# Two dense blocks on one core: three seams between products computed by token halves

## The reference, cut to what matters

```
x    += 0.5 * gate * swiglu(ada_norm(x))        # ffn 0, for latent and context
x    += gate * mixer(ada_norm(x))               # layer 0: even mixer, layer 1: odd mixer
x    += 0.5 * gate * swiglu(ada_norm(x))        # ffn 1
ada_norm(x) = x * rsqrt(mean(x*x) + eps) * g * (1 + scale) + shift
swiglu(h)   = (silu(h @ Wa) * (h @ Wb)) @ Wout
```

## Time and profile before

| | |
|---|---|
| median of 3 runs | 2419.37 us (2418.14 to 2423.27) |
| the profiled execution | 2423.33 us, its span 2421.5 us |
| TensorE, VectorE, ScalarE, GpSimd busy | 95%, 48%, 36%, 6% |
| mean granted TensorE clock | 0.973 |

### The profile page before, as it was taken

One profiled execution on the slowest core, in us unless ns is written; L12 is line 12 of the kernel. 1 busy time (PEld: TensorE's weight loads), 2 busy tenths in 40 slices (PEclk: granted clock), 3 DMA queues, 4 the chain that ended last, 5 costly groups with the idle time before them and its releaser, 6 DMA issues.

```text
span 2421.5 us, 35525 instructions
## 1 busy us (share of the span) xinstructions
PE 2310.0 (95%) x13280; PEld 1863.4 (77%) x13280; DVE 1156.7 (48%) x1943; ACT 876.3 (36%) x1399; POOL 154.0 (6%) x134
## 2 busy tenths in 40 slices
PE   6999999999999999988999999999999998988998
PEld 4777797877777778856777777778788876968998
DVE  5226375643433353376553333354343345566665
ACT  4126454632222232346443222244222234355544
POOL 0003112100000010040200000010000010000000
PEclk9999999999999999988999999999999998998999
DMA  9652543445555245400344665333233232323573
GB/s 304 198 165 81 179 133 79 148 122 173 179 178 176 86 119 155 124 9 27 105 148 146 196 183 157 104 109 94 72 117 90 79 105 69 88 70 113 164 207 116
DMA packets 514685, 312.87 MB, mean 129 GB/s; under 512 B 15899, under 2 KB 513138, under 8 KB 514454
## 3 DMA queue, kind: packets, MB, share of 16 engines
q1 hardware_dynamic: 513992, 311.33, 43.5%
q10 hardware_dynamic: 590, 0.16, 0.0%
HBM read 310.41 MB, written 1.05 MB: 129 GB/s over the span
## 4 chain that ended last, share of the span: by engine, by line
PE 86%; DVE 7%; ACT 3%; issue 2%; DMA 1%; ACTq 0%; POOL 0%; DVEq 0%; POOLq 0%
PE ps L907 68%; PE ps L949 4%; PE ps L717 4%; DVE w_lo L1551 2%; PE ps L1793 1%; ACT w_hi L1168 1%; PE ps L859 1%; PE ps L1772 1%; PE ps L2114 1%; PE ps L1780 1%; PE ps L790 1%; PE ps L811 0%; PE ps L2010 0%; DVE small L2286 0%; PE ps L728 0%
## 5 line engine op out<-in xcount | busy, mean ns | idle before, releaser
L907 PE MATMUL ps<-h_hi,w_hi 128*128 128x512 f32 (+1 forms) x2208 | 806.5, 365 | 28.3 <-DVE h_lo L1408 14.1
L907 PE MATMUL ps<-h_lo,w_hi 128*128 128x512 f32 (+1 forms) x2208 | 793.0, 359 | 0.0
L907 PE MATMUL ps<-h_hi,w_lo 128*128 128x512 f32 (+1 forms) x2208 | 792.9, 359 | 0.0
L907 PEld LDWEIGHTS ps<-h_hi,w_hi 128*128 128x128 f32 x2208 | 420.9, 191 | 126.5 <-issue 48.4
L1551 DVE TENSOR_TENSOR w_lo<-stage,w_hi 128x1024 fp32r<-128x1024 f32 x227 | 284.0, 1253 | 403.3 <-ACT w_hi L1168 402.8
L907 PEld LDWEIGHTS ps<-h_hi,w_lo 128*128 128x128 f32 x2208 | 421.0, 191 | 67.9
L907 PEld LDWEIGHTS ps<-h_lo,w_hi 128*128 128x128 f32 x2208 | 421.6, 191 | 63.7
L1168 ACT ACTIVATE w_hi<-stage 128x1024 fp32r<-128x1024 f32 x227 | 237.0, 1055 | 360.9 <-PE ps L907 245.7
L1551 DVE TENSOR_TENSOR w_lo<-deep,w_hi 128x1024 fp32r<-128x1024 f32 x184 | 225.4, 1234 | 274.5 <-ACT w_hi L1168 273.3
L907 PE MATMUL ps<-g_hi,w_hi 128*128 128x512 f32 (+1 forms) x704 | 260.2, 370 | 0.6 <-DVE w_lo L1551 0.3
L907 PE MATMUL ps<-g_hi,w_lo 128*128 128x512 f32 (+1 forms) x704 | 257.4, 366 | 0.0
(11 more groups left out here) (368 smaller groups left out, 2381.8 us busy)
## 6 DMA issues: line engine op xcount, KB each, us to landing
modw<-in_ada_w SPq DMA_DIRECT2D x72, 1024.0 KB, 5.6
stage<-in_ffn_w_in SPq DMA_DIRECT2D x88, 512.0 KB, 4.5
deep<-in_ffn_w_in SPq DMA_DIRECT2D x88, 512.0 KB, 3.8
modw<-in_w_mod SPq DMA_DIRECT2D x18, 1024.0 KB, 7.8
stage<-in_w_in SPq DMA_DIRECT2D x30, 512.0 KB, 4.7
stage<-in_ffn_w_out SPq DMA_DIRECT2D x32, 384.0 KB, 3.4
stage<-in_even_w_in SPq DMA_DIRECT2D x24, 512.0 KB, 4.0
deep<-in_ffn_w_out SPq DMA_DIRECT2D x32, 384.0 KB, 3.5
```

Of the source, the lines that this page charges most:

```text
L907: last = mm(ps[:, j, 0:b - a], w_part[wp][:, u % RING, c, :], x_part[xp][:, x, a:b], start=first and wp == xp, stop=final and wp == "lo")
```

## The change

The phase `seam` takes the place of the last two output chunks of the old projection, of the norm and of the first four units of the new one. The old chunks j=6 and 7 are computed for the latent half, then for the context half (which alone raises `unit_done`). During the context half the latent sums of squares and rstd are computed. Then the four new units run for the latent half, the second pair q=1 interleaved with chunks 4 to 7 of the first pair q=0, and after that for the context half. VectorE and ScalarE get one written order each with evacuations, weight splits and norm chunks; the latent norm issues scaled(c+1) after low(c), the context norm ahead of it. The gemm before a seam has six output chunks (its sums include a sixth square), the one after it begins four units later. The first gemm of the even mixer hosts its modulation segments in half as many units, another takes two more, the ffn's two fewer. `deep` now starts with the first new unit of seam 3.

```diff
+        def seam(tail, start, norm, dst=None):
+            units = 2 * len(tail["ks"]) + 4
+            r = {"unit_done": units, "w_hi": units, "w_ready": units, "x_done": 2, "sq_half": 4, "ms_sum": 2, "rms_ready": 2, "diag_ready": 2,
+                 "rstd_ready": 2, "t_ready": 2 * KC, "hi_ready": 2 * KC, "h_ready": 2 * KC, "bank_free0": 1, "bank_free1": 1, "bank_free2": 3, "bank_free3": 3}
+            if dst is None:
+                r.update({"x_done": 4, "sg_half": 4, "gh_hi": 4, "g_half": 2, "g_ready": 2})
+            add("seam", r, start=start, norm=norm, dst=dst, **tail)
+        def ffn(i, nt, hpers, after=None):
...
-                     sumsq="resid" if half else None, fed=not (last and i and half), peel=i and half, hper=hpers[2 * half + 1])
+                w_down = dict(w=("ffn_w_out_2", l, i), src="g", ks=(6, 5), row0=half * FH, l=l, g=2 * i)
+                if half and after:
+                    gemm(w_down.pop("w"), 0, KC - 2, "resid", tok=(0, nt), sumsq="early", **w_down)
+                    after(dict(w=("ffn_w_out_2", l, i), **w_down))
+                else:
+                    gemm(w_down.pop("w"), 0, KC, "resid", tok=(0, nt), sumsq="resid" if half else None,
+                         fed=not (last and i and half), peel=i and half, hper=hpers[2 * half + 1], **w_down)
+        w = ("even_w_in_2", 0) if l == 0 else ("odd_w_in_2", 0)
+        def into_even(tail):
+            modvec(1, 0, (1, 2))
+            seam(tail, w, (0, 1), dst=0)
+        def into_last(tail):
+            modvec(1, 1, (0, 1, 2))
+            seam(tail, ("ffn_w_in_2", 1, 0), (1, 0))
 
...
-            gemm(w, 0, 8, "copy", dst=0, hper=2)
+            gemm(w, 512, 4, "copy", dst=4, hper=4)
             add("rotary", {"roped": 1, "lam_e": 1}, half=0)
             gemm(w, 1024, 2, "tok", dst="vda")
             add("rotary", {"roped": 1}, half=1)
-            gemm(w, 1536, 4, "copy", dst=8, hper=2)
+            gemm(w, 1536, 4, "copy", dst=8, hper=4)
...
-            gemm(("even_w_out_2", 0), 0, 8, "resid", l=l, g=1, sumsq="resid")
+            tail = dict(src="h", ks=(KC,), row0=0, l=l, g=1)
+            gemm(("even_w_out_2", 0), 0, KC - 2, "resid", sumsq="early", **tail)
+            seam(dict(w=("even_w_out_2", 0), **tail), ("ffn_w_in_2", 0, 1), (0, 2))
...
+        def tn_of(v, c):
+            return tn[:, c % 6, :] if v == 0 else big3[:, 11 + 12 * (c // 2 % 2), c % 2 * SEQ:c % 2 * SEQ + SEQ]
...
-        first_deep = next(p.at("unit_done") for p in phases if p.kind == "gemm" and p.at("mod_rows") == total["mod_rows"] and p.kw["ks"] == (KC,))
+        first_deep = next(p.at("unit_done") for p in phases if p.kind == "seam" and p.at("mod_rows") == total["mod_rows"]) + 4
...
+        def sp_seam(eng, p):
+            k, u0 = p.kw, p.at("unit_done")
+            w_out, w_in = (weight(w).rearrange("(k p) n -> p k n", p=P) for w in (k["w"], k["start"]))
+            u = u0
+            for j in (6, 7):
+                for s, kc in enumerate(k["ks"]):
+                    first = k["row0"] + sum(k["ks"][:s])
+                    slot, full, _, again = arrival(u)
+                    eng.wait_ge(S("w_ready"), u - again + 1)
+                    eng.dma_start(slot[:, 0:kc, :], w_out[:, first:first + kc, j * P:j * P + P]).then_inc(full, 16)
+                    u += 1
+            if u == first_deep:
+                eng.wait_ge(S("mod_rows"), total["mod_rows"])
+            for j in range(4):
+                col = j * P if k["dst"] is not None else j // 2 * P + j % 2 * D_FF
+                slot, full, _, again = arrival(u)
+                eng.wait_ge(S("w_ready"), u - again + 1)
+                eng.dma_start(slot[:, :, :], w_in[:, 0:KC, col:col + P]).then_inc(full, 16)
+                u += 1
...
+        def pe_seam(eng, p):
+            k, u0 = p.kw, p.at("unit_done")
+            ks, per = k["ks"], len(k["ks"])
+            w_part, x_part = {"hi": w_hi, "lo": w_lo}, {"hi": h_hi, "lo": h_lo}
+            t_part = x_part if k["src"] == "h" else {"hi": g_hi, "lo": g_lo}
+            def sums(v):
+                if v == 0:
+                    for name in ("mod_sum", "mod_kept"):
+                        eng.wait_ge(S(name), p.at(name))
+                    eng.wait_ge(S("sq_used"), p.at("sq_used"))
+                eng.wait_ge(S("sq_half"), p.at("sq_half", 2 * v + 2))
+                cols = slice(v * SEQ, (v + 1) * SEQ)
+                up(pe_half_sums(v, [sqsum[:, cols], sq[:, 0, cols], sq[:, 1, cols]], True, True), "ms_sum")
+            for v in range(2):
+                cols = slice(v * SEQ, (v + 1) * SEQ)
+                for j in range(2):
+                    eng.wait_ge(S(f"bank_free{2 + j}"), p.at(f"bank_free{2 + j}", v))
+                    for s, kc in enumerate(ks):
+                        u = u0 + j * per + s
+                        if v == 0:
+                            eng.wait_ge(S("w_ready"), u + 1)
+                        for n in range(kc):
+                            x = sum(ks[:s]) + n
+                            for wp, xp in W_X:
+                                last = mm(ps[:, 2 + j, cols], w_part[wp][:, u % RING, n, :], t_part[xp][:, x, cols],
+                                          start=x == 0 and wp == xp, stop=x == sum(ks) - 1 and wp == "lo")
+                            if v and j * sum(ks) + x == 3:
+                                sums(0)
+                            if v and j * sum(ks) + x == 8:
+                                pe_half_rstd(eng, p, 0, 1)
+                        if v:
+                            up(last, "unit_done")
+                    if v == 0:
+                        up(last, "x_done")
+            u1 = u0 + 2 * per
+            turn = [(0, n) for n in range(4)] + [(q, n + 4 * (1 - q)) for n in range(4) for q in (1, 0)] + [(1, n) for n in range(4, KC)]
+            for v in range(2):
+                cols = slice(v * SEQ, (v + 1) * SEQ)
+                for q, n in turn:
+                    if q == 0:
+                        eng.wait_ge(S("h_ready"), p.at("h_ready", KC * v + n + 1))
+                    for j in range(2):
+                        u = u1 + 2 * q + j
+                        bank, part = (2 * q + v, slice(j * SEQ, (j + 1) * SEQ)) if k["dst"] is None else (2 * q + j, cols)
+                        if n == 0:
+                            if v == 0:
+                                eng.wait_ge(S("w_ready"), u + 1)
+                            eng.wait_ge(S(f"bank_free{bank}"), p.at(f"bank_free{bank}", 2 * (bank // 2)))
+                        for wp, xp in W_X:
+                            last = mm(ps[:, bank, part], w_part[wp][:, u % RING, n, :], x_part[xp][:, n, cols],
+                                      start=n == 0 and wp == xp and (k["dst"] is not None or j == 0), stop=n == KC - 1 and wp == "lo", skip_group_check=True)
+                        if n == KC - 1 and v and k["dst"] is not None:
+                            up(last, "unit_done")
+                    if n == KC - 1 and k["dst"] is None:
+                        up(last, "unit_done", by=2) if v else up(last, "x_done")
+                    if v == 0 and (q, n) == (0, 3):
+                        sums(1)
+                    if v == 0 and (q, n) == (0, 6):
+                        pe_half_rstd(eng, p, 1, 2)
...
+        def seam_splits(p):
+            return ((4,), (5,), (), (6, 7)) if len(p.kw["ks"]) == 2 else ((4,), (), (), (5,))
+        def act_seam(eng, p):
+            k, u0 = p.kw, p.at("unit_done")
+            u1 = u0 + 2 * len(k["ks"])
+            m = 2 + k["norm"][0]
+            def square(v, j):
+                eng.wait_ge(S(f"bank_free{2 + j}"), p.at(f"bank_free{2 + j}", v + 1))
+                cols = slice(v * SEQ, (v + 1) * SEQ)
+                up(act(sq[:, j, cols], resid[:, 6 + j, cols], ACT.Square), "sq_half")
+            def high(v, c):
+                eng.wait_ge(S("t_ready"), p.at("t_ready", KC * v + c + 1))
+                up(act(h_hi[:, c, v * SEQ:(v + 1) * SEQ], tn_of(v, c), ACT.Identity, bias=modT[m][:, k["norm"][1] * 24 + c, v:v + 1], scale=1.0), "hi_ready")
+            def gate(v, q):
+                cols = slice(v * SEQ, (v + 1) * SEQ)
+                eng.wait_ge(S("unit_done"), u1 + 2 * q + 2) if v else eng.wait_ge(S("x_done"), p.at("x_done", 3 + q))
+                up(act(sg[:, q, cols], ps[:, 2 * q + v, 0:SEQ], ACT.Silu), "sg_half")
+            def keep(j):
+                eng.wait_ge(S("unit_done"), u1 + j + 1)
+                up(act(big3[:, k["dst"] + j, :], ps[:, j, :], ACT.Copy), f"bank_free{j}")
+            act_split(eng, u0 + 3)
+            act(small[:, 212:213], epsc[:, :], ACT.Sqrt)
+            eng.wait_ge(S("sq_used"), p.at("sq_used"))
+            square(0, 0)
+            square(0, 1)
+            act_half_root(eng, p, 0, 1)
+            for c in range(KC):
+                if c < 4:
+                    for s in seam_splits(p)[c]:
+                        act_split(eng, u0 + s)
+                high(0, c)
```

(90 more changed lines are left out.)

37 lines of the change are left out of this document (16 added, 21 removed).

## The result

Four runs of each: 2435.73 us after (2433.45 to 2440.13) against 2420.96 before (2418.14 to 2423.27). The ratio is 1.0064, 95% interval 1.0045 to 1.0083: slower by 0.64%. Forecast was 2432.9 us, +13.5; measured +14.8. The profiled execution of the kernel after took 2440.13 us, its span 2438.3.

A forecast was written before the change was run, and what follows sets the result against it. TensorE, busy 95%, bounds the kernel; only seam gaps, 27.9 us, can be won. New work 11.55 + 1.2, stalls 23.1 and clock 5.6 make 41.4, so +13.5: 2432.9 us. Range 2416 to 2441, likeliest case 2425 to 2439.5.

The forecast's parts named there:

- The old cost and TensorE's own work: Three seams: old gaps and slow matmuls 27.9 us; new sums and rstd 11.55, halves 1.2; worth 15.2 without stalls.
- The stalls of the walk: TensorE waits at the seams from the VectorE and ScalarE queue order: 6.5 + 9.2 + 7.4 = 23.1 us.
- The fourth chunk: Chunk 3 of the latent norm, behind weight splits it does not need: stalls 4.25, 1.85, 2.95 us in seams 1 to 3.
- the bank: Seam 2, old units' context half: bank 2 evacuated only behind the split of u0+3, stall 2.3 us.
- the ends: After seams 2 and 3 the next product waits for weights whose ring slots come free late: 2.15 us each.
- Chunks 4 and 5: Latent norm chunks after the second sums, root and diagonal: stalls of 1.4, 1.35 and 1.4 us.
- The clock: Half clock after stalls: 1.6 us each for two, 0.8 each for three, 5.6 in all, bounds 0 and 14.
- the price from the earlier trace: In a late product, after a 2.52 us wait, 18 half matmuls take 3.75 us instead of 2.12, 1.63 lost.
- (a): Rival: the splits hide, queues keep up at chunk 3; sum +1.2, 2420.6 us, no change; chance 0.15.
- (b): Rival: faster, weight splits outside TensorE's path; -7.7, 2411.7 us, or 2404 with no wait left; chance 0.13.
- (c): Rival: all five stalls draw the dearest clock loss and segments cost 2; +24, 2443.4 us; chance 0.08.
- The segments: Seam 1's modulation segments, four per four units instead of two: up to 2 us if delaying a weight, taken at 0.

The follow-up runs named there:

- all orders: Kernel after with end and bank edits, weight splits just ahead of the weight's own use, one chunk scaled ahead: 2409.78 us, ratio 0.9965 to before.
- three edits: Each alone on the kernel after: weight splits behind the fourth chunk 2424.15 us; straight order at the end 2430.98; bank ahead of the split in seam 2 2432.90.
- seam 2 alone: Only the second seam runs by halves, the other two as in the kernel before: 2427.21 us, ratio 1.0024 to before.
- splits behind: Kernel after with the weight splits moved behind the fourth chunk's high and low parts: 2424.15 us, ratio 1.0018 to before.
- two kernels with reads: All orders plus, per seam, two or four VectorE reductions nobody reads, ahead of the second chunk's low op: 2414.75 us (two), 2419.68 (four).
- three small edits: Kernel after with splits behind the fourth chunk, straight order at the end and bank ahead of the split together: 2420.06 us, ratio 0.9998 to before.
- seam 3 alone: Only the third seam runs by halves, the other two as in the kernel before: 2422.25 us, ratio 1.0010 to before.
- seam 1 alone: Only the first seam runs by halves, the other two as in the kernel before: 2424.28 us, ratio 1.0022 to before.
- bank first: Kernel after, latent halves evacuated before the fourth weight's split in seam 2, ScalarE's root table loaded after the squares: 2432.90 us, ratio 1.0052 to before.
- straight end: Kernel after with the new units' context half running pair q=0 to its last chunk, then q=1: 2430.98 us, ratio 1.0044 to before.

## Why the prediction was right, and where it was not

**The old cost and TensorE's own work: right.** 27.9 us of old gaps and slow matmuls, against 11.55 + 1.2 of new work. Twelve sums matmuls hold up the next product 1.25 us (878.83, the row itself is 1.45 long) for the 1.36 forecast, halves start 0.118 us apart. The kernel with all orders checks it: 468 x 0.233 = 109.0, + 12.75 of work, + 3.0 of waits makes 124.8, and eight of its waits cost 0.16 us more than the row says, because a matmul's row is 0.28 long while the next starts 0.118 later: 126.1 against 126.6 measured. The sum holds better than its terms: the rstd matmuls take 0.25 us each in all orders instead of 0.52, so sums and rstd come to 9.3 us instead of 11.55, and in their place stand some 2.8 us of pauses of 0.1 to 0.2 us at single halves, too short for the list of waits. So halves were worth the forecast 15.2 us, less the waits.

**The stalls of the walk: right in place, a little large.** The fourth chunk 3.65, 1.43 and 2.56 us (forecast 4.25, 1.85, 2.95), the bank 2.02 (2.3), the ends 2.01 and 2.01 (2.15 each), none at the end of seam 1. The first chunks 0.50, 0.97 and 0.48 (0.85, 1.55, 0.9). Together 15.6, and 17.2 with 0.16 for each of the ten rows, against 18.95 forecast. That the order of the queue is their cause is shown: each of three edits moves operations without removing one, and the waits that it aims at go, but for 0.49 us at the fourth chunk of seam 2 and 0.26 at its sums. Of the three, only the splits' worth in time is clear of noise.

**Chunks 4 and 5: wrong in the kernel after.** 1.4, 1.35 and 1.4 us were forecast and none is there. The clock hid them: TensorE was then at its lower level and used a chunk in 2.6 us instead of 1.41. Where the clock stays up they come: 0.51 + 0.35 us in seam 2 alone, for the 1.35 forecast. (With the splits behind, seam 1 has 0.22 + 0.82 there, but in that kernel two splits stand ahead of these chunks.) The two kernels with reads agree: seam 1 has 0.24 + 0.16 us of waits there with two reads, at full clock, and none with four, at the lower.

**The clock: the term that was mis-sized.** Forecast 5.6 us: 1.6 for two stalls, 0.8 for three. Half matmuls and sums ran slow for some 27.5 us, at 0.213 instead of 0.118 each, which loses 12.2; with 1.4 and 1.5 at the ends 15.1. The step that failed is the price from the earlier trace rows, 18 half matmuls in 3.75 us, as the dear end: the stall of 2.56 in seam 3 was followed by nearly 9 us at the lower level, seam 1's and seam 2's bank wait by 8 and 7, and 1.43 us, which had got no clock term, also dropped it. Too much for chunks 4 and 5 (4.15), too little for the clock (9.5): the two errors are one thing counted in two places, and half cancelled.

**Sum.** 12.75 + 17.2 + 15.1 = 45.1, where the lengths show 153.0 - 109.0 = 44.0 and the forecast had 41.4; the 1.1 us between are not explained. Against the 137.2 of before the lengths give +15.8, against +13.5 forecast and +14.8 measured.

**The rivals.** (a), the splits hide, fell: moving them gave 11.6 us. (b), faster, did not hold for this order; but its floor of 2404 was a fair one, for with the order mended the time is 2409.8. Its point of decision, stalls and clock under 15.2, is borne out by all orders (some 5 us, faster). The three small edits have 11.9 in the profiled execution and should by it be 3 us faster; their interval, -3.4 to +2.2, does not tell that from no change. Of "against" one reason was too strong: ring slots are freed by the context half alone, and yet the order inside that half mends the wait. (c) was nearest in the size of the clock's part, 14.1 against 15.1: the loss was larger than its 2.83 us in three places, about 1.5 at the two ends, and a sixth place that it left out, the fourth chunk of seam 2, lost 1.5.

**The segments.** Taken at nothing, and not nothing. The stretch between seams 2 and 3, which hosts 26 segments instead of 28, is 366.0 to 366.3 us long, slow ends left out, in every kernel that runs seam 2 by halves, against 368.7, 368.7 and 369.2 in the three that do not. The stretch between seams 1 and 2, which hosts ten instead of eight, is 277.0 to 280.3 us in every kernel with all seams by halves, against 273.3 before and 271.8 with seam 3 alone. Some 4 us more and 2.5 less is a net loss of about 2 us in the kernel after, as much as the prediction named as the most. The number of segments does not explain the first stretch: seam 1 alone hosts eight there, as before, and still has 276.6. What does stays open. These microseconds stand outside the seams' lengths. Ahead of seam 1, where nothing was changed, the kernels differ by up to 5.8 us (its start is at 869.1 to 874.8), so a single stretch of a single execution says little; it is the agreement of the kernels that does.

## What to carry to other kernels

When a product is split so that an engine's list can run beside it, write down for each operation in the list which TensorE instruction needs it, and issue in that order: here the same instructions cost +14.8 us or gained 10.9 by their order alone. A weight split of 1.2 us ahead of a 0.4 us op that TensorE awaits is the first thing to look for. Price a stall with the clock that it can take with it (here from nothing to some 4 us for waits of 0.8 to 3.7), and do not add a stall that would only occur at full clock.

## What the runs showed of the hardware

The same wait does not take the same clock with it. After a wait of 1.42 us at the fourth chunk of seam 2 the clock stays at 1.00 when that seam alone runs by halves (the wait, then the window behind it), and in the kernel with the bank first it reads 0.50 for the five microseconds from 1217 on (the last two lines). In the kernel after, 1.43 us at the same place took three microseconds at 0.50 with it. What TensorE did before differs: in the first it had waited 2.02 us nearly fifteen microseconds earlier, had run at 0.50 for three microseconds behind that, and had waited twice for half a microsecond since; in the second 0.26 us and twice for half a microsecond, at full clock.

```profile
1218.80 0.38 PE L989 MATMUL ps<-h_hi,w_hi 128*128 128x256 f32 x1 [1.42 <-DVE h_lo L1733]
```

```profile
1219.00:1224.00 5.00, 4.44 (x36) 1.00 0.90 276
```

```profile
1216.30 0.58 PE L970 MATMUL ps<-h_hi,w_hi 128*128 128x256 f32 x1 [1.42 <-DVE h_lo L1714]
```

```profile
1217.00:1222.00 5.00, 5.00 (x24) 0.50 0.99 306
```

At seam 3 a wait of 2.55 or 2.56 us was followed by nearly nine microseconds at 0.50 in the kernels after and bank first, and by only three in the one with the straight end, where the clock is up again after them:

```profile
1638.00:1641.00 3.00, 3.00 (x15) 0.50 0.62 178
1642.00:1645.00 3.00, 3.00 (x25) 1.00 0.00 0
```

The Trainium skill, TensorE: Matmul & The Clock Gate, part 1, calls the throttled state the default and reports a kernel with 6, 11 or 14 cold matmuls from run to run, counted from the kernel's start. The runs here, behind waits in mid-stream, agree in kind and are wider: none, or some 10 to 30 half matmuls at the lower level (and up to twelve of the sums), after like waits. In the kernel with all orders, where no wait in a seam is over 0.78 us, the clock stayed up in all three, as it did with three waits of 1.2 to 1.3. In the kernel with three small edits it fell in seam 1 with no wait over 0.83, and stayed up in seam 3 of the same execution after nearly the same row of waits (0.50, 0.50, 0.15 and 0.83 against 0.48, 0.48, 0.15 and 0.82 us). For each seam, the last wait and a stretch behind it:

```profile
894.61 0.54 PE L971 MATMUL ps<-h_hi,w_hi 128*128 128x256 f32 x1 [0.83 <-DVE h_lo L1718]
895.00:898.00 3.00, 3.00 (x16) 0.50 1.09 350
...
1626.92 0.38 PE L971 MATMUL ps<-h_hi,w_hi 128*128 128x256 f32 x1 [0.82 <-DVE h_lo L1718]
1627.00:1631.00 4.00, 3.66 (x29) 1.00 0.60 168
```

So the length of a wait does not decide alone. What else does is not settled by these runs.
